# The halves' exchange of the rotary turn on ScalarE instead of TensorE, in a two-block transformer step on one core

## The reference

```python
def apply_rope(x, tables):
    cos, sin = tables
    cos, sin = cos[None, :, None, :], sin[None, :, None, :]
    x1, x2 = jnp.split(x, 2, axis=-1)
    return jnp.concatenate([x1 * cos - x2 * sin, x2 * cos + x1 * sin], axis=-1)
...
    q = rms_norm(q.reshape(B, S, GQA_HEADS, GQA_HEAD_DIM), q_gain)
    k = rms_norm(k.reshape(B, S, GQA_KV_HEADS, GQA_HEAD_DIM), k_gain)
...
        q = apply_rope(q, rope_gqa)
        k = apply_rope(k, rope_gqa)
        q_rope = apply_rope(q_rope, rope_mla)
        kr = apply_rope(kr, rope_mla)
```

## Time and profile before

| | |
|---|---|
| Time, median of 3 runs | 3330.27 us (3326.84 to 3333.37) |
| Time of the profiled execution | 3327.34 us |
| Its span | 3325.5 us, 38664 instructions |
| PE busy | 2998.3 us (90%) |
| DVE busy | 2492.4 us (75%) |
| ACT busy | 1174.1 us (35%) |
| POOL busy | 704.6 us (21%) |
| Chain that ended last, by engine | PE 66%, DVE 12%, DMA 8%, issue 5%, POOL 5%, ACT 2% |
| Mean granted TensorE clock | 0.957 |

### The profile page before, as it was taken

How to read it: one execution, slowest core, us unless ns; L and a number is a source line. 1 busy time by engine, 2 the same in 40 slices (tenths; PEclk the granted TensorE clock), 3 DMA queues, 4 the chain that set the end, 5 groups by cost and what they waited for, 6 DMA issues and landing times.

```text
span 3325.5 us, 38664 instructions
## 1 busy us (share of the span) xinstructions
PE 2998.3 (90%) x14668; PEld 2290.7 (69%) x14668; DVE 2492.4 (75%) x3460; ACT 1174.1 (35%) x1804; POOL 704.6 (21%) x748
## 2 busy tenths in 40 slices
PE   5899999999999999998999999899999997666666
PEld 1577887546777898578999899788888885222223
DVE  7888996655877777468664563798988996888876
ACT  1332323324234444145544554344444442111111
POOL 1000000000320000014000000222122224777773
PEclk9999999999999999999999999999999998878878
DMA  9554675252876686538444444899999999999996
GB/s 407 212 190 190 237 268 203 104 213 91 315 277 238 256 323 234 221 142 333 154 162 142 165 157 148 325 409 417 404 413 407 416 400 358 388 409 409 409 409 264
DMA packets 160233, 932.69 MB, mean 280 GB/s; under 512 B 21553, under 2 KB 42289, under 8 KB 53169
## 3 DMA queue, kind: packets, MB, share of 16 engines
q0 software_dynamic: 77568, 520.24, 39.7%
q1 hardware_dynamic: 68368, 384.82, 29.7%
q10 hardware_dynamic: 14112, 25.17, 2.0%
HBM read 900.79 MB, written 29.36 MB: 280 GB/s over the span
## 4 chain that ended last, share of the span: by engine, by line
PE 66%; DVE 12%; DMA 8%; issue 5%; POOL 5%; ACT 2%; DVEq 0%; SPq 0%; ACTq 0%; POOLq 0%
PE psum L1150 31%; PE psum L1095 17%; PE psum L1159 6%; DMA memh<-dots,memr 3%; PE psum L1301 3%; DVE w_lo L1437 3%; POOL memr L969 2%; PE psum L1119 2%; POOL memh L957 2%; PE psum L1320 2%; DVE psum L2383 2%; DMA memr<-in_panels_dram 2%; DMA memh<-in_panels_dram 1%; DVE junk L1927 1%; PE psum L1342 1%
## 5 line engine op out<-in xcount | busy, mean ns | idle before, releaser
L1437 DVE TENSOR_TENSOR w_lo<-memr,w_hi 128x1024 fp32r<-128x1024 f32 x614 | 744.1, 1233 | 330.5 <-ACT w_hi L1430 330.1
L1430 ACT ACTIVATE w_hi<-memr 128x1024 fp32r<-128x1024 f32 x614 | 642.5, 1057 | 873.4 <-PE psum L1150 383.9
L1150 PE MATMUL psum<-h_hi,w_hi 128*128 128x512 f32 (+1 forms) x1632 | 576.9, 354 | 6.6 <-DVE w_lo L1437 6.0
L1927 DVE CUSTOM_DVE_ANT_0 junk<-memr 128x2048 bf16<-128x2048 f32 x224 | 520.6, 2324 | 75.5 <-DMA memr<-in_ada_dram 54.9
L1150 PE MATMUL psum<-h_hi,w_lo 128*128 128x512 f32 (+1 forms) x1632 | 562.0, 344 | 0.0
L1150 PE MATMUL psum<-h_lo,w_hi 128*128 128x512 f32 (+1 forms) x1632 | 561.7, 344 | 0.0
L1342 PE MATMUL psum<-memr,memh 128*128 128x512 f32 x576 | 317.5, 711 | 187.6 <-ACT memh L1863 170.2
L1095 PE MATMUL psum<-w_hi,l_hi 128*128 128x512 f32 x1024 | 400.0, 391 | 12.9 <-DVE w_lo L1437 12.8
L1095 PE MATMUL psum<-w_hi,l_lo 128*128 128x512 f32 x1024 | 399.6, 390 | 0.0
L1095 PE MATMUL psum<-w_lo,l_hi 128*128 128x512 f32 x1024 | 399.4, 390 | 0.0
L1342 PEld LDWEIGHTS psum<-memr,memh 128*128 128x128 f32 x576 | 127.2, 229 | 377.4 <-ACT memh L1863 183.7
(11 more groups left out here) (275 smaller groups left out, 4381.8 us busy)
## 6 DMA issues: line engine op xcount, KB each, us to landing
memr<-in_panels_dram SPq DMA_DIRECT2D x323, 1024.0 KB, 7.5
memr<-in_ada_dram POOLq DMA_DIRECT2D x168, 1024.0 KB, 5.2
memh<-in_panels_dram SPq DMA_DIRECT2D x16, 1024.0 KB, 22.9
dots<-sq ACTq DMA_DIRECT2D x64, 256.0 KB, 9.5
memh<-in_ada_dram POOLq DMA_DIRECT2D x8, 1024.0 KB, 16.1
memr<-in_xin_dram SPq DMA_DIRECT2D x1, 4096.0 KB, 41.4
gstore<-sq ACTq DMA_DIRECT2D x16, 256.0 KB, 4.8
memh<-gstore SPq DMA_DIRECT2D x2, 2048.0 KB, 7.4
```

Source lines behind the costliest of these rows:

```text
L1150: ins = pe.matmul(bank(o["bank"])[:, 0:o["w"]], w_[:, c, :], x_[:, kc, :], start=kc == 0 and j == 0, stop=kc == DC - 1 and j == 2)
L1430: act.activation(hi, a, ACT.Copy).then_inc(hi_ready, 1)
L1437: dve.tensor_tensor(lo_, a, hi.bitcast(F32), ALU.subtract).then_inc(lo_ready, 1)
L1927: chain(dve.tensor_tensor_reduce(junk[:, :], w, cact[:, v_, :], 1.0, 0.0, ALU.mult, ALU.add, mod[:, a, m:m + 1]))
```

## The change

For the groups without `pair` (the 8 query and 2 key heads of each layer) the product on PE is left out. ACT makes the exchange with two copies from SBUF to the same PSUM bank, each from one half of the partitions to the other half. The steps, the bank, the semaphores and their counts stay; the waits for `roped` and `normed` go over to ACT. `kr` keeps its product on PE.

```diff
@@ pe_inside
-                if gr.get("swap_at") == step:
-                    if gr["sw"]:
-                        pe.wait_ge(roped, gr["sw"])
-                    if gr.get("stat", True):
-                        pe.wait_ge(normed, gr["ms"] + 1)
-                    else:
-                        pe.wait_ge(evac[gr["made"][0]["eng"]], gr["made"][0]["ev"] + 1)
-                    pe.matmul(bank(SWAP_BANK)[:, 0:S], con("swap2" if gr["pair"] else "swap", P), gr["rope"],
-                              start=True, stop=True).then_inc(swapped, 1)
+                if gr.get("swap_at") == step and gr["pair"]:
+                    pe.wait_ge(roped, gr["sw"])
+                    pe.wait_ge(evac[gr["made"][0]["eng"]], gr["made"][0]["ev"] + 1)
+                    pe.matmul(bank(SWAP_BANK)[:, 0:S], con("swap2", P), gr["rope"], start=True, stop=True).then_inc(swapped, 1)
@@ act_inside, between the square and the root of a group
+                if gr.get("swap_at") == step and not gr["pair"]:
+                    if gr["sw"]:
+                        act.wait_ge(roped, gr["sw"])
+                    act.wait_ge(normed, gr["ms"] + 1)
+                    act.activation(bank(SWAP_BANK)[0:64, 0:S], gr["rope"][64:P, :], ACT.Copy)
+                    act.activation(bank(SWAP_BANK)[64:P, 0:S], gr["rope"][0:64, :], ACT.Copy).then_inc(swapped, 1)
```

## The result

The changed kernel takes 3338.07 us, median of 9 runs (3334.54 to 3343.35), against 3330.27 us for the kernel before (9 runs beside it, 3321.15 to 3334.34). The ratio is 1.0031 with the interval [1.0023, 1.0039]: slower, by 7.7 to 13 us. Forecast was 3331, no change; rival B, the clock, was priced at 3338 and given 0.13.

The account below looks back on a forecast made before the run. TensorE (PE) was taken as the bound, busy 2998 of 3325.5 us. Layer 1 loses 1.8 us, layer 0 gains 1.1: 0.7 slower, 3328.0 from the profiled execution, 3331 against the median; range 3318 to 3340.

Parts of the forecast that it names:

- rival B: Layer 1's five chained steps each get a slow clock start of 1.4 us: 7.7 us slower, 3338; chance 0.13.
- steps 11 to 15: Layer 1, one projection output per step: PE's sum waits through ScalarE, period 8.6 us instead of 7.59, costing 5.0 us.
- The moved wait: ScalarE, not PE, waits for DVE's turn; the root queues behind, so PE's sum comes 0.9 to 1.0 us later (layer 1).
- The price of the copies: Two 64 x 256 ScalarE copies per exchange: 0.28 us each until the next starts, 0.56 together, bounds 0.28 and 0.82.
- r to S: From the end of DVE's turn to the start of a step's sum on PE: 1.50 us in layer 1, 1.92 in layer 0.
- rival C: Copies dear (over 0.5 us each, no overlap, or partition crossing): 0.5 us per step in 11 steps, 3336; within the forecast's 0.67.
- Layer 1, step by step: Layer 1's projection: 5.0 us lost in chained steps, less gains of 1.0, 0.4, 1.4 and 0.4: 1.8 us lost.
- step 16: Layer 1: its sum is the second of `cq`, so PE is free of the turn; gain 1.41 us.
- The two waits around `kr`: Layer 1: one long wait instead, `kr`'s exchange 2.6 us earlier, slow products moved to step 8; gain 1.0, bounds 0 and 2.6.
- Layer 0: Layer 0's projection, all steps together: a gain of 1.1 us, bounds 2.6 and -0.5.
- Steps 6 to 10: Layer 0: sums about 12.05 us apart, 0.2 less than now; five steps gain 1.0 us.
- step 11: Layer 0: DVE's modulation chunks set the turn, and PE's sum waits for it through ScalarE; 1.3 us lost.

Follow-up runs that it names:

- experiment 7: The changed kernel with ten extra products on PE before the sum's wait in steps 11 to 15 of layer 1: 3328.46 us, ratio 1.0.
- experiment 5: The changed kernel with ScalarE's roots before the exchange copies, and `kr`'s exchange also on ScalarE by four 32 x 256 copies: 3307.35 us, ratio 0.9939.
- experiment 3: The changed kernel with the exchange on ScalarE in layer 1 only; layer 0 keeps its product on PE: 3337.94 us, ratio 1.0032.
- experiment 8: The changed kernel with two 64 x 256 copies that leave each half in its place, so no exchange: 3336.32 us, one run.
- Experiments 2: The changed kernel with twenty extra products on PE before the sum's wait in steps 11 to 15 of layer 1: 3327.4 us, ratio 0.9998.
- experiment 1: The changed kernel with ScalarE doing all squares and roots of a step before the exchange copies: 3313.62 us, ratio 0.9958.
- Experiment 6: The changed kernel with the exchange on ScalarE in layer 0 only; layer 1 keeps its product on PE: 3328.53 us, ratio 1.0.
- experiment 4: The changed kernel with one straight 128 x 256 copy for the two half copies, leaving the exchange out: 3333.09 us, ratio 1.0012.

## Why the prediction was wrong

**The step that failed** is the weighing of the clock, in "Rivals, B": the sum went without slow starts, and the rival with them got 0.13. The prediction had the gap ("from 0.72 us to about 2.3 in each period"); it measured 2.40. It had the price ("a start at 1.4 us" in each of five steps); it measured 5 x 1.49. What it got wrong was whether such gaps slow the clock. Against it stood one row, the granted clock of 1.00 after a gap of 2.95 us in layer 1's attention. That row was one draw of a case that goes either way. In experiment 7, at the same place and in the same stretch of time, PE waited 3.10 us, and the clock fell; timeline of PE, then the stretch with its clock of 0.74:

```profile
1296.22 0.63 PE L1314 MATMUL psum<-consts,sq 128*128 128x128 f32 x4 [3.10 <-DVE sq L2118]
```

```profile
1294.00:1300.00 6.00, 3.78 (x15) 2.65 (x16) 1.96 (x6) 3.20 (x8) 0.00 (x0) 0.74 0.77 276
```

Seven of the ten kernels have a gap of 2.68 to 3.43 us there, and behind four of them, also in the kernel after (2.73 us), the clock went to 0.50 for 3.4 us; behind 3.39 us in experiment 5 it didn't. In the loop of steps 11 to 15 it fell behind all fifteen gaps of 2.40 us (kernel after, experiments 3 and 8). So a single gap without a slow start could not carry the weight that it got. Experiments 2 and 7 show the clock as the cause of 1.49 us a step: the same waits with products in the gap give 8.84 us a step and the level of 2.4 GHz. What decides whether the clock falls behind a gap of this size, the traces don't show. The Trainium skill, TensorE: Matmul & The Clock Gate, section A second HAM failure mode: psum-queue depth-cycling, says of another kernel that frequent short idles of PE between groups of products make the clock oscillate between its two levels and that the cost is paid between the bursts. The traces agree with the first at gaps of 2.40 and 1.90 us in every step (clock 0.86 and 0.89), not at gaps of 1.20 (1.00); and the cost is paid here inside the group, where products go 0.21 us apart from about 1 us behind its start.

That the median of 3338.07 us meets the 3338 of rival B so closely is in part luck. B's sum was 7.7 us; the steps of the profiles add to 13.1 (below).

**The moved wait**: right. The root stands behind the wait for the turn, and PE waits for the root; experiment 1, which changes that alone, takes some 24 us off the changed kernel.

**The price of the copies**: too low. 0.28 us each until the next may start was the term; they take 0.39 (to the second copy) and 0.41 (to Ln), 0.80 instead of 0.56, close to the upper bound of 0.82. From r to S it is 1.74 us instead of the forecast 1.50 (0.1 for the restart comes on top in both), and a step without slow products is 8.84 us instead of 8.6; over five steps that is 1.2 us. Of rival C's three conditions one came, no overlap, and at half of C's price (0.24 us a step dearer, not 0.5); no copy took over 0.5 us, and crossing cost nothing. Of the overlap that the prediction cites from the Trainium skill, ScalarE: Activation LUTs, section What ACT_TABLE_LOAD costs, the one copy on 128 partitions shows 0.07 us (0.32 us from its start to Ln's, at a length of 0.39); the two half copies show none (0.39 us apart at 0.38, then 0.41 to Ln at 0.39).

**Layer 1, step by step.** From before's 1102.15 to 1147.70 and after's 1099.53 to 1157.48 (steps 11 to 16) it is 57.95 us instead of 45.55. That is 5 x 1.25 for the chain, 5 x 1.49 for the clock, less 1.30 at step 16 (forecast 1.41): 12.4. Steps 10 and 17 give 0.25 and 0.43, against 0.43 each. The two waits around `kr` became one of 4.96 us as forecast, and its exchange came at 1078.55 instead of 1082.65, 4.1 us earlier, of which 1.8 was gained before. The slow products behind that wait went into step 8, as forecast (1079.56 to 1087.00, 7.44 us instead of 6.18); the gain there was 0.5, within the bounds of 0 and 2.6 around the 1.0 that was taken. In all the profiled stretch from step 5 to step 17 is 11.2 us longer (forecast 1.8).

**Layer 0.** Steps 6 to 10 last 12.20 to 12.32 instead of 12.05 (forecast) and 12.23 (before); step 11 lost 1.6 (forecast 1.3) and then another 1.3 for slow products behind a gap of 3.57 us, which the forecast had not. The profile has 1.9 us lost where a gain of 1.1 was forecast. Experiment 6, whose interval reaches from 3.0 us below the kernel before to 3.0 above, can't tell either from nothing.

**What stays open.** By the steps, the profiles have 11.2 + 1.9 = 13.1 us of loss, and the spans differ by 14.1; the medians lie 7.8 apart, in an interval from 7.7 to 13. Experiments 2 and 7 should by their steps be some 5 us slower than the kernel before, and their medians are 1.8 and 0.2 us below it (intervals up to 2.3 and 3.0 above). So some 5 to 7 us by the medians, and at least 2 to 3 by the intervals, are given back elsewhere. The spans hide this, since the rest outside the two projections nearly cancels. Compared at the starts of the same DVE instructions, the profile of the kernel after gains 3.3 us on that of before between 800 and 1000 us, between the two projections, and loses 1.7 between 1250 and 1310 us (with the slow start in the attention) and 3.5 between 1400 and 1600. In the first of these stretches each of the nine other kernels gains 3.3 to 5.0 us on the one profile of before, experiment 3 too, which up to there runs the same instructions. One wait for a remainder of the weights makes 2 us of it: 4.70 us in the kernel before, 2.45 to 2.68 in the nine others. PE's timeline of the kernel before and of the kernel after:

```profile
846.13 0.80 PE L1150 MATMUL psum<-h_hi,w_hi 128*128 128x512 f32 x1 [4.70 <-DVE w_lo L1437]
```

```profile
845.35 0.50 PE L1145 MATMUL psum<-h_hi,w_hi 128*128 128x512 f32 x1 [2.66 <-DVE w_lo L1432]
```

Whether the kernel before always loses this or lost it in that execution alone, one profile of it can't tell.

## What to carry to other kernels

Before a wait is moved to another engine, look at what stands behind it in that engine's queue in the same step. If the old owner waits for one of those, nothing is freed; put what the others wait for ahead of the new wait, and the same change turned from 0.3% slower into 0.4% faster. And where a wait returns in every step of a loop on TensorE, price it with and without a slow start of the clock. A single gap elsewhere in the run that left the clock up is no evidence against it: here gaps of 2.68 to 3.43 us at one and the same place did so in three profiles of seven.

## What the runs showed of the hardware

- The clock in a loop with one gap per step, over the five gaps of layer 1: with 1.20 us (steps of 8.84 us, experiment 7) it stood at 1.00; with 1.90 us (experiment 4) it was 0.89 over 48 us, with slow starts behind the second to the fourth gap; with 2.40 us (kernel after) it was 0.86, with a slow start behind each, also in experiments 3 and 8. There the slow products began 0.9 to 1.2 us after PE had resumed (1109.61 behind 1108.37).
- Behind a single gap of 2.68 to 3.43 us in layer 1's attention the clock fell to 0.50 for 3.4 us in four profiles of seven. The length doesn't order them: it fell behind 2.73 us (kernel after) and not behind 3.39 (experiment 5).
- 1.49 us is lost at each slow start of the loop, though PE's idle time itself didn't grow by it: the half copies, and with them the turn, come later by as much.
- A copy of 64 x 256 on ACT takes 0.38 us whether or not it crosses partitions (kernel after, experiment 8), and one of 128 x 256 within its own partitions takes 0.39 us (experiment 4). Two half copies start 0.39 us apart.
